# A one-core encoder block: the variance of the convolution's norm by four full products instead of sixteen one-column products, a diagonal and a spread

## The reference

```python
def layernorm(x, w, b):
    xf = x.astype(jnp.float32)
    mu = jnp.mean(xf, axis=-1, keepdims=True)
    var = jnp.mean(jnp.square(xf - mu), axis=-1, keepdims=True)
    y = (xf - mu) * lax.rsqrt(var + EPS)
    return y * w.astype(jnp.float32) + b.astype(jnp.float32)

def conformer_conv_group(proj_a, proj_b, conv_w, conv_b, ln_w, ln_b):
    u = proj_a * jax.nn.sigmoid(proj_b)
    ...
    y = layernorm(y, ln_w, ln_b)
    return jax.nn.silu(y).astype(proj_a.dtype)
```

## Time and profile before

| what | us |
|---|---|
| median of 3 runs | 2952.61 (2951.25 to 2954.43) |
| the profiled execution's own time | 2954.14 |
| its span | 2952.2 |
| TensorE busy in the span | 2821.5 (96%) |
| VectorE busy | 1366.0 (46%) |
| GpSimd busy | 888.6 (30%) |
| ScalarE busy | 549.1 (19%) |

### The profile page before, as it was taken

How to read it: one execution, slowest core, us unless ns; L and a number is a source line. 1 busy time by engine, 2 the same in 40 slices (tenths; PEclk the granted TensorE clock), 3 DMA queues, 4 the chain that set the end, 5 groups by cost and what they waited for, 6 DMA issues and landing times.

```text
span 2952.2 us, 37368 instructions
## 1 busy us (share of the span) xinstructions
PE 2821.5 (96%) x14050; PEld 2388.8 (81%) x14050; DVE 1366.0 (46%) x1534; ACT 549.1 (19%) x950; POOL 888.6 (30%) x443
## 2 busy tenths in 40 slices
PE   5899999996898999999999999989999999999998
PEld 4788888885887898888888888778988888888887
DVE  4593939496765433532514224443335324142343
ACT  5211111112354322100100001232221000010012
POOL 1242524333872100233323333310003233333331
PEclk8999999998889999999999999999999999999999
DMA  4133333336644222111111113232231111111111
GB/s 158 50 111 125 104 114 118 120 114 224 211 144 156 93 86 86 50 50 50 43 49 50 45 48 107 64 107 88 83 95 43 50 50 43 50 50 49 44 50 71
DMA packets 289755, 254.01 MB, mean 86 GB/s; under 512 B 8016, under 2 KB 253960, under 8 KB 283400
## 3 DMA queue, kind: packets, MB, share of 16 engines
q1 hardware_dynamic: 266320, 203.45, 22.3%
q10 hardware_dynamic: 23352, 49.39, 4.5%
HBM read 196.71 MB, written 56.10 MB: 86 GB/s over the span
## 4 chain that ended last, share of the span: by engine, by line
PE 77%; DVE 14%; DMA 3%; issue 2%; ACT 2%; POOL 1%; DVEq 0%; ACTq 0%; SPq 0%; POOLq 0%
PE ps L681 22%; PE ps L676 21%; PE ps L677 21%; DVE acc L1651 10%; PE ps L1036 2%; PE ps L1038 2%; PE ps L1037 2%; PE ps L900 1%; PE ps L828 1%; DMA wqk_d<-pst 1%; PE ps L998 1%; DVE alo L1938 1%; DMA out<-rows 1%; PE ps L1047 0%; DMA wb<-wqk_d 0%
## 5 line engine op out<-in xcount | busy, mean ns | idle before, releaser
L537 POOL TENSOR_SCALAR whi<-wraw 128x1024 fp32r<-128x1024 f32 x192 | 231.0, 1203 | 1903.9 <-PE ps L681 1186.5
L676 PE MATMUL ps<-ahi,whi 128*128 128x512 f32 x1376 | 542.3, 394 | 17.4 <-DVE alo L1938 11.6
L677 PE MATMUL ps<-alo,whi 128*128 128x512 f32 x1376 | 537.8, 391 | 0.0
L539 POOL TENSOR_TENSOR wlo<-wraw,whi 128x1024 fp32r<-128x1024 f32 x192 | 529.8, 2760 | 16.0
L676 PE MATMUL ps<-bhi,whi 128*128 128x512 f32 x1024 | 399.4, 390 | 2.3 <-DVE blo L1859 2.3
L677 PE MATMUL ps<-blo,whi 128*128 128x512 f32 x1024 | 398.4, 389 | 0.0
L1651 DVE SCALAR_TENSOR_TENSOR acc<-upad,taps,acc 128x2048 f32<-128x2048 f32 x120 | 346.6, 2888 | 15.7 <-DVE acc L1648 0.6
L681 PE MATMUL ps<-ahi,wlo 128*128 128x512 f32 x1376 | 340.2, 389 | 0.0
L676 PE MATMUL ps<-xhi,whi 128*128 128x512 f32 x768 | 305.5, 398 | 18.7 <-DVE xlo L1582 11.2
L676 PEld LDWEIGHTS ps<-ahi,whi 128*128 128x128 f32 x1376 | 259.5, 189 | 78.3 <-DVE alo L1938 14.9
L677 PE MATMUL ps<-xlo,whi 128*128 128x512 f32 x768 | 303.7, 395 | 0.0
(11 more groups left out here) (264 smaller groups left out, 3637.1 us busy)
## 6 DMA issues: line engine op xcount, KB each, us to landing
wraw<-in_w_ff SPq DMA_DIRECT2D x128, 512.0 KB, 3.9
proj_d<-st ACTq DMA_DIRECT2D x64, 256.0 KB, 2.5
wraw<-in_w_in SPq DMA_DIRECT2D x24, 512.0 KB, 4.7
xt<-in_x SPq DMA_DIRECT2D x16, 512.0 KB, 6.7
wraw<-in_w_xkv SPq DMA_DIRECT2D x16, 512.0 KB, 5.6
vwo_d<-pst ACTq DMA_DIRECT2D x16, 512.0 KB, 3.7
wqk_d<-pst ACTq DMA_DIRECT2D x16, 512.0 KB, 4.1
wraw<-in_w_out SPq DMA_DIRECT2D x16, 512.0 KB, 5.1
```

The costliest lines, as they stand in the source:

```text
L537: pool.tensor_scalar(whi[:, slot, :, :], wraw[:, slot, :, :], 1.0, 0.0, ALU.mult, ALU.add).then_inc(w_hi, 1)
L539: pool.tensor_tensor(wlo[:, slot, :, :], wraw[:, slot, :, :], whi[:, slot, :, :], ALU.subtract).then_inc(w_ready, 1)
L676: nc.tensor.matmul(o, whi[:, slot, k, :], hi(k), start=(k == order[0]), stop=False)
L677: nc.tensor.matmul(o, whi[:, slot, k, :], lo(k), start=False, stop=False)
```

## The change

The variance is summed by four products of `mean_mat` with the squares, 512 columns wide, into bank 3, which leave it on every partition. The root and the reciprocal are taken of 128x512 instead of 128x4, in SBUF. The diagonal and the spread are gone, and `conv_norm` multiplies by `cr` in SBUF instead of by bank 3. `conv_vars` waits for all four centrings before its first product, since bank 3 still holds the mean; `chunk_states` and `first_mix` wait for the root instead of for the multiplications before they reuse bank 3.

```diff
-            diag = b2("diag", (P, 4, P))
+            cr = b2("cr", (P, NC))
...
-            cr = b2("cr", (P, 4))
...
                 for i in range(4):
-                    if h and i == 2:
+                    if h and i == 3:
                         pe.wait_ge(c_std, h)
-                    if h and i == 3:
-                        pe.wait_ge(c_mul, CT * h)
...
             def conv_vars(h):
 
+                pe.wait_ge(c_cen, CT * h + CT)
                 for c in range(CT):
                     pe.wait_ge(c_sq, CT * h + c + 1)
-                    for t in range(4):
-                        last = pe.matmul(ps[:, 2, t:t + 1], cv_w[:, c % 2, t * P:(t + 1) * P], mean_mat[:, 0:1],
-                                         start=(c == 0 and t == 0), stop=(c == CT - 1 and t == 3))
-                    last.then_inc(c_va, 1)
-
-            def conv_spread(h):
-
-                pe.wait_ge(c_dg, h + 1)
-                pe.wait_ge(c_cen, CT * h + CT)
-                pe.matmul(ps[:, 3, :], mean_mat[:, :], diag[:, :, :].rearrange("p c q -> p (c q)"), start=True, stop=True).then_inc(c_bc, 1)
+                    pe.matmul(ps[:, 3, :], mean_mat[:, :], cv_w[:, c % 2, :], start=(c == 0), stop=(c == CT - 1)).then_inc(c_va, 1)
...
-                    if (s, n) == (1, 0):
+                    if (s, n) == (1, 1):
                         pe.wait_ge(c_std, HEADS)
-                    if (s, n) == (1, 1):
-                        pe.wait_ge(c_mul, CT * HEADS)
...
-                        conv_spread(HEADS - 1)
...
-                act.activation(cr[:, :], ps[:, 2, 0:4], ACT.Sqrt, bias=eps[:, :], scale=P / CW).then_inc(c_std, 1)
+                act.activation(cr[:, :], ps[:, 3, :], ACT.Sqrt, bias=eps[:, :], scale=P / CW).then_inc(c_std, 1)
...
-            def conv_diagonal(h):
+            def conv_recip(h):
 
                 dve.wait_ge(c_std, h + 1)
                 dve.reciprocal(cr[:, :], cr[:, :]).then_inc(c_rc, 1)
+
+            def conv_norm(h):
+
                 dve.wait_ge(c_rc, h + 1)
-                dve.scalar_tensor_tensor(out=diag[:, :, :], in0=ident[:, :].unsqueeze(1).to_broadcast([P, 4, P]), scalar=float(P),
-                                         in1=cr[:, :].unsqueeze(2).to_broadcast([P, 4, P]), op0=ALU.mult, op1=ALU.mult).then_inc(c_dg, 1)
-
-            def conv_norm(h):
-
-                dve.wait_ge(c_bc, h + 1)
                 for c in range(CT):
-                    dve.tensor_tensor(cvs[h % 2][:, c, :], cvs[h % 2][:, c, :], ps[:, 3, :], ALU.mult).then_inc(c_mul, 1)
+                    dve.tensor_tensor(cvs[h % 2][:, c, :], cvs[h % 2][:, c, :], cr[:, :], ALU.mult).then_inc(c_mul, 1)
```

More of the change, by code:

```diff
@@ L277, in build @@
         c_in = [sem("c_in0"), sem("c_in1")]
-        c_me, c_cen, c_sq, c_va, c_std, c_rc, c_dg, c_bc, c_mul, c_out, c_st = (
-            sem(n) for n in ("c_me", "c_cen", "c_sq", "c_va", "c_std", "c_rc", "c_dg", "c_bc", "c_mul", "c_out", "c_st"))
+        c_me, c_cen, c_sq, c_va, c_std, c_rc, c_mul, c_out, c_st = (
+            sem(n) for n in ("c_me", "c_cen", "c_sq", "c_va", "c_std", "c_rc", "c_mul", "c_out", "c_st"))
         y_in = [sem(f"y_in{k}") for k in range(KT)]
@@ L930, in _ @@
                     value_tokens(h + 1)
-                    conv_spread(h)
                     turn_back(h)
@@ L1836, in _ @@
                     split_low(0, [5, 6, 7])
-                conv_diagonal(h)
+                conv_recip(h)
                 conv_norm(h)
```

## The result

| | us | runs |
|---|---|---|
| before, median | 2953.6 (2950.39 to 2958.61) | 14 |
| changed, median | 2959.65 (2954.73 to 2963.04) | 14 |
| ratio | 1.0021, 95% interval 1.0013 to 1.0028 | |
| changed, the profiled execution | 2957.81, span 2955.7 | 1 |

The change makes the kernel 0.21% slower, 6.05 us by the medians. The forecast was 2959.5.

A forecast was written before the change was run, and what follows sets the result against it. TensorE is busy 96% of the span, with VectorE's scan nearly on its path in the second stage. 2.0 + 1.9 + 3.4 + 1.9 - 2.4 = +6.8 on the profiled 2954.14 gave 2960.9, by median 2959.5; range 2947 to 2966.

The forecast's parts named there:

- Multiplications in turns: In `conv_norm`, two-SBUF-input multiplications alternate with GpSimd products, delaying the scan: +2.0 us head 0, +3.4 head 1, +1.3 head 2.
- The reciprocal: On VectorE ahead of the multiplications: 3.3 us for 128x512, one SBUF input, not blocked by GpSimd.
- The scan on the path, head 2 covered: VectorE's forward scan has 0.14 us slack, so TensorE pays delays; head 2's loss (1.3 + 1.9) hides behind the `y_stage` transfer.
- The clock lost in the gaps: TensorE idling ahead of the scores drops to half clock: +1.9 us for each of heads 0 and 1.
- The clock in head 0: Forecast: returns some 3.7 us after 772.6 under wide variance products. Rival: it doesn't, 2956.9 us; chance 0.29 with smaller terms.
- The last head: Spread gone between output products and turning back at better clock: -2.4 us, at least 1.0 and at most 3.6 gained.
- The faster rivals: VectorE's multiplications wait less for GpSimd or not at all, so the kernel gets faster: 2943 or 2938.5 us; chance 0.14.
- multiplications that keep GpSimd out: In `conv_norm`, only the first multiplication waits for GpSimd, the other three follow directly: -9.7 us, 2943.
- nothing excludes anything: VectorE and GpSimd never block each other, early `chunk_states` count in full: -14.1 us, 2938.5.

The follow-up runs named there:

- e1: Changed kernel with the reciprocal written to bank 3 of `ps`, from where the four multiplications read it: 2943.88 us against 2952.43 before.
- e2: Changed kernel with GpSimd's two k products each issued as four pieces of 512 columns: 2949.55 us, 0.9988 of before.
- e9: Kernel before, unedited, run again for a second trace: 2953.28 us, stage 171.1 us.
- e10: Kernel before, unedited, run again for a third trace: 2950.07 us, stage 170.6 us.
- e3: Changed kernel with the reciprocal taken of 4 columns instead of 512: 2960.26 us, 1.0028 of before.
- e7: Changed kernel with the reciprocal written to bank 3 of `ps` and taken of 4 columns instead of 512: 2942.46 us, 0.9965 of before.
- e5: Kernel before with an unused 3.35 us VectorE reciprocal behind `conv_norm` in heads 0 to 2, delaying the scan: 2958.88 us against 2953.93.
- e4: Kernel before with one unused full product added behind each tile's four one-column products, after waiting for all four centrings: 2962.95 us, 1.0038 of before.

## Why the prediction was right

**Multiplications in turns: right in kind and size.** Each waits for a GpSimd product and ends 0.55 us behind it. The end in head 1 was forecast at 835.7 and the scan there 3.5 us late. Measured from the last retained product of the head before, the scores are late by 2.07 us in head 0 (35.77 less 33.70; forecast 2.0), 3.19 in head 1 (28.47 less 25.28; forecast 3.4), and 0.91 in head 2 (forecast 1.3). e1 and e2 show the cause. Against e9 and e10, in which before had more clock, head 1 is 4.3 late, so the agreement of the single terms owes something to the trace they were worked out from.

**The reciprocal: right.** 3.35 us, and GpSimd's product across it took its usual time. e3 and e7 show that it costs nothing that can be measured: most of it is covered by the wait for GpSimd in heads 0 and 1, by the half clock and `y_stage` behind them (e3), or by the room that the early values leave (e7).

**The scan on the path, head 2 covered: right.** e5, with the delay alone, pays 4.95 us for two heads of 2.4 to 2.8 us each and nothing for the third. In the changed kernel head 2 loses 2.29 us (44.39 less 42.10) and gains it back: ScalarE waits 4.13 us for `y_stage` where it waited 6.64:

```profile
900.15 1.06 ACT L1378 ACTIVATE ahi<-y_stage 128x1024 fp32r<-128x1024 f32 x1 [4.13 <-DMA y_stage<-y_d]
```

**The clock lost in the gaps: right in kind, 1.9 was too much.** It falls in both gaps, and the scores lose 1.45 and 1.42 us (from the scores' start to the end of the retained products: 19.41 and 19.38 against 17.96). I had taken half of the 3.8 us in which the clock had come back elsewhere; here it was back some 3 us behind the start of the scores (at 798.3 and 846.1), and half of that was lost.

**The clock in head 0: the rival did not come.** It came back at 774.5 under the full products, about when forecast. One argument given against that rival misreads the rows: the value products are of 128 columns, a quarter of the new width and not half. What one-column products do to the clock is shown by the pair of before and changed kernel, and by heads 1 and 2 of e4; that wide products bring it back whatever stands between them is not so (e4, head 0).

**The last head: mis-sized.** Forecast -2.4, bound -3.6. From `y_stage`'s arrival to the residual it was 41.35 us (935.44 less 894.09) and is 37.73 (937.88 less 900.15): -3.6, the bound. The agreement with the bound is luck, since its parts are others. I had counted 1.0 for the spread and at best 1.8 for the turning back. Measured from `y_stage`'s arrival, the turning back starts 1.7 us earlier (12.75 behind it, where it was 14.44), because the variance's products too ran at full clock, a term that I had left out; the turning back gives 1.65, and from the first output product on, where the spread stood, only 0.3 is gained.

**The sum.** 2.07 + 1.45 + 3.19 + 1.42 - 3.84 = 4.3 for the first pair of traces (-3.84 is -6.13, the last head as a whole, with the 2.29 of head 2 set against it as covered), where I had 6.8. The 2.5 between them: the clock's loss forecast 0.9 too large, the last head's gain 1.4 too small, the late scans 0.1 too large. That the median still came out at the forecast is luck, a second error that went the other way: the trace of before that I counted from had 2.2 us more in the stage than the mean of three. I counted its half-clock stretches as fixed, and they vary by 3.4 us each.

**The faster rivals.** e1 took 2943.88, close to the 2943 stated for multiplications that keep GpSimd out, but it is not that case: its four multiplications take 2.48 us and wait for nothing. It is the other one, in which nothing excludes anything and the early states count in full, stated as 14.1 us less (3.4, 4.7, 3.6 and 2.4 by heads) and 2938.5. Against the first trace of before, e1's heads are 3.4, 4.3, 3.2 and 1.9 us shorter, 12.8 in all, so those terms were nearly right; by the medians it is 8.5, for the reason just given and because executions differ outside the stage.

The Trainium skill, SBUF — State Buffer, section Who interferes with whom, names the two-input VectorE instruction as the one that contends with GpSimd; the sixteen multiplications of the changed kernel agree (median 1.75 us against 0.68 with one operand in `ps`).

## What to carry to other kernels

Where GpSimd runs long products, an operand that VectorE multiplies with again and again belongs in the accumulator, even if an instruction has to write it there: here 3.35 us of reciprocal into `ps` made the same four multiplications 2.5 instead of 8.7 and 11.2 us (heads 0 and 1), and turned a change that cost 6 us into one that gains 8.5. That is shown for this kernel alone. If it must stay in SBUF, shorter GpSimd pieces shorten the turns (e2). And a difference of a few microseconds is taken from several traces of both kernels, stage by stage, since one trace's clock may not be typical.

## What the runs showed of the hardware that I had not expected

- Back-to-back VectorE instructions and waiting GpSimd products alternate one by one, however close the VectorE ones stand: saving 3.17 us ahead of them (e3) moved their end by 1.2.
- With full products between one-column ones the clock stayed up in heads 1 and 2 (e4, 785.3 to 904.4 at 1.00), and did not rise where it was down (764.7 to 785.0, TensorE busy for 16.37 of 20.30 us; 904.7 to 918.2, busy throughout). Why the same mix does one and not the other is open.
- Idle gaps of 2.39, 2.72 and 2.38 us ahead of the scores left the clock alone (e5); those of 4.96, 7.43 and 4.01 us in the changed kernel did not.
- In identical runs of before, the half clock around the variance lasted 10.2 or 6.8 us in head 1 and 6.8 or 3.4 us in head 2.
